# Seven more pieces of the sample rows' attention values split into a rounded part and its rest, one per prompt column, on one Trainium2 core

## What is computed

```python
def cross_attention(h, mem_k, mem_v, w_q, w_o):
    B, T, _ = h.shape
    q = jnp.einsum('btd,de->bte', h, w_q).reshape(B, T, XA_HEADS, XA_HD)
    s = jnp.einsum('bthd,bmhd->bhtm', q, mem_k.astype(h.dtype)).astype(jnp.float32) * (XA_HD ** -0.5)
    p = jax.nn.softmax(s, axis=-1).astype(h.dtype)
    o = jnp.einsum('bhtm,bmhd->bthd', p, mem_v.astype(h.dtype)).reshape(B, T, D_MODEL)
    return jnp.einsum('btd,de->bte', o, w_o)
```

## Time and profile before

| | us |
|---|---|
| median of 3 runs | 1855.91 |
| lowest, highest | 1854.45, 1859.5 |
| the profiled execution | 1854.26 |
| its span, first to last instruction | 1851.9 |
| TensorE busy in the span | 1814.0 |
| VectorE busy | 1150.0 |
| ScalarE busy | 796.2 |
| mean granted TensorE clock | 0.998 of full |

### The profile page before, as it was taken

One profiled execution on the slowest core, in us unless ns is written; L12 is line 12 of the kernel. 1 busy time (PEld: TensorE's weight loads), 2 busy tenths in 40 slices (PEclk: granted clock), 3 DMA queues, 4 the chain that ended last, 5 costly groups with the idle time before them and its releaser, 6 DMA issues.

```text
span 1851.9 us, 34219 instructions
## 1 busy us (share of the span) xinstructions
PE 1814.0 (98%) x13818; PEld 1723.1 (93%) x13818; DVE 1150.0 (62%) x1573; ACT 796.2 (43%) x842; POOL 183.2 (10%) x185
## 2 busy tenths in 40 slices
PE   8999999999999999999999999999999999999997
PEld 6999999988999999888749999999999999999997
DVE  6888447746766577555676656666544566665443
ACT  6454545343363533443642344443333444443344
POOL 5000000002106300000005500000000000000231
PEclk9999999999999999999999999999999999999999
DMA  8555554472045667797784688886456899984553
GB/s 266 162 166 174 180 167 155 137 241 76 17 154 177 216 211 247 276 311 250 251 283 128 190 239 249 250 249 193 129 183 193 239 249 248 249 225 134 170 187 110
DMA packets 415128, 367.19 MB, mean 198 GB/s; under 512 B 11519, under 2 KB 374014, under 8 KB 414486
## 3 DMA queue, kind: packets, MB, share of 16 engines
q1 hardware_dynamic: 387368, 340.76, 60.0%
q10 hardware_dynamic: 27678, 25.26, 4.2%
HBM read 347.84 MB, written 18.35 MB: 198 GB/s over the span
## 4 chain that ended last, share of the span: by engine, by line
PE 89%; DVE 5%; ACT 2%; issue 1%; POOL 1%; DMA 1%; DVEq 0%; ACTq 0%; POOLq 0%
PE ps L467 65%; PE ps L543 9%; PE ps L524 4%; DVE w_lo L446 2%; PE ps L961 1%; PE ps L510 1%; PE ps L1245 1%; ACT w_hi L439 1%; PE ps L1260 1%; PE ps L1163 1%; PE ps L1084 1%; PE ps L1402 1%; DMA gst<-in_state_gla_dram 1%; PE ps L1448 1%; PE ps L1440 1%
## 5 line engine op out<-in xcount | busy, mean ns | idle before, releaser
L439 ACT ACTIVATE w_hi<-raw 128x2048 fp32r<-128x2048 f32 (+1 forms) x285 | 512.3, 1797 | 857.6 <-PE ps L467 709.9
L446 DVE TENSOR_TENSOR w_lo<-raw,w_hi 128x2048 fp32r<-128x2048 f32 (+1 forms) x285 | 620.1, 2176 | 261.3 <-ACT w_hi L439 258.1
L467 PE MATMUL ps<-act_hi,w_lo 128*128 128x264 f32 x2560 | 732.8, 286 | 6.2 <-DVE w_lo L446 4.1
L467 PE MATMUL ps<-act_lo,w_hi 128*128 128x264 f32 x2560 | 725.4, 283 | 0.0
L467 PE MATMUL ps<-act_hi,w_hi 128*128 128x264 f32 x2560 | 724.9, 283 | 0.0
L467 PEld LDWEIGHTS ps<-act_hi,w_lo 128*128 128x128 f32 x2560 | 482.2, 188 | 10.6 <-issue 3.9
L467 PEld LDWEIGHTS ps<-act_lo,w_hi 128*128 128x128 f32 x2560 | 482.5, 188 | 0.4
L467 PEld LDWEIGHTS ps<-act_hi,w_hi 128*128 128x128 f32 x2560 | 480.0, 187 | 0.0
L467 PE MATMUL ps<-ff_hi,w_lo 128*128 128x264 f32 x704 | 201.1, 286 | 0.0
L467 PE MATMUL ps<-ff_hi,w_hi 128*128 128x264 f32 x704 | 200.1, 284 | 0.0
L467 PE MATMUL ps<-ff_lo,w_hi 128*128 128x264 f32 x704 | 199.4, 283 | 0.0
(11 more groups left out here) (444 smaller groups left out, 2172.9 us busy)
## 6 DMA issues: line engine op xcount, KB each, us to landing
raw<-in_w_in_dram SPq DMA_DIRECT2D x56, 1024.0 KB, 7.5
raw<-in_ffn_w_gate_dram SPq DMA_DIRECT2D x44, 1024.0 KB, 5.7
raw<-in_ffn_w_up_dram SPq DMA_DIRECT2D x44, 1024.0 KB, 5.7
raw<-in_ffn_w_down_dram SPq DMA_DIRECT2D x32, 768.0 KB, 4.8
raw<-in_ffn_w_down_dram SPq DMA_DIRECT2D x32, 640.0 KB, 6.1
raw<-in_w_out_dram SPq DMA_DIRECT2D x16, 1024.0 KB, 6.3
raw<-in_xa_w_q_dram SPq DMA_DIRECT2D x16, 1024.0 KB, 6.7
raw<-in_xa_w_k_dram SPq DMA_DIRECT2D x16, 1024.0 KB, 6.3
```

What stands on the lines that cost most here:

```text
L439: act.activation(w_part(ph, w_hi[b]), raw_part(ph, r, half), ACT.Copy)\
L446: dve.tensor_tensor(w_part(ph, w_lo[b]), raw_part(ph, r, half), w_part(ph, w_hi[b]), ALU.subtract)\
L467: mm = pe.matmul(ps[:, acc(ph, u), 0:ph.cols], w[b][:, k, :], v[:, kk + k, 0:ph.cols], start=first and k == 0 and m == 0, stop=last and k ...
```

## The change

`HALVED` goes from 18 to 25, so pieces 18 to 24, the first seven of the tail, take the split form too; a new name, `EARLY_HALVED`, keeps the old 18. VectorE no longer makes the rounded copy `ow_hi` of the 16 prompt tiles: ScalarE does, in a loop over j of its own. For each j that loop has `first_values(18 + j)`, a wait for `att_o` (tile j summed by TensorE), the copy `ow_hi`, and for j up to 6 `high_values(18 + j)`. VectorE waits for that copy before `ow_lo`, and for j up to 6 does `low_values(18 + j)` behind it. The copy of `orow` now stands at j = 15 of ScalarE's loop.

```diff
--- before.py
+++ after.py
@@ -59,7 +59,8 @@
 EARLY_PIECES = 14
 RING = 8
 PIECES = 2 * NB * XH
-HALVED = 18
+EARLY_HALVED = 18
+HALVED = 25
 ACC_CREDIT = 4
 
 
@@ -2031,13 +2032,18 @@
                         high_values(2 * (n - 39) + v)
                 if n == 3 * KT - 1:
                     keep_rows(3, 1)
-            for v in range(18, NB * XH):
-                if v == 20:
+            for j in range(KT):
+                if j == 2:
                     split(*unit_at(3 * KT + 1))
-                first_values(v)
-            W(act, "s_o", NB * XH)
-            act.activation(orow[:, :], ps[0:NB * XH, 6, :], ACT.Copy).then_inc(rows_copied, 1)
-
+                if j < 14:
+                    first_values(18 + j)
+                if j == KT - 1:
+                    W(act, "s_o", NB * XH)
+                    act.activation(orow[:, :], ps[0:NB * XH, 6, :], ACT.Copy).then_inc(rows_copied, 1)
+                W(act, "att_o", j + 1)
+                act.activation(ow_hi[:, j, 0:T], ps[:, 4 + j % 2, 0:T], ACT.Copy).then_inc(v_halved, 1)
+                if EARLY_HALVED + j < HALVED:
+                    high_values(EARLY_HALVED + j)
             run("x_o", none, "gu0")
             act.wait_ge(new_rows_kept, 32)
             run_with_pieces(0, gate_take, "dn0")
@@ -2634,7 +2640,7 @@
 
             def low_values(n):
 
-                dve.wait_ge(v_halved, n + 1)
+                dve.wait_ge(v_halved, n + 1 + max(n + 1 - EARLY_HALVED, 0))
                 r = (NB * XH + n - EARLY_PIECES) % RING
                 dve.tensor_tensor(ring_r[r][:, 0, :], ring[r][:, 0, :], ring_r[r][:, 1, :], ALU.subtract).then_inc(v_mixed, 1)
 
@@ -2685,8 +2691,10 @@
                        .then_inc(N["s_oe"], 1)
                 W(dve, "att_o", j + 1)
                 src = ps[:, 4 + j % 2, 0:T]
-                link(dve.tensor_copy(ow_hi[:, j, 0:T], src))
+                dve.wait_ge(v_halved, EARLY_HALVED + j + 1 + min(j, HALVED - EARLY_HALVED))
                 dve.tensor_tensor(ow_lo[:, j, 0:T], src, ow_hi[:, j, 0:T], ALU.subtract).then_inc(N["att_oe"], 1)
+                if EARLY_HALVED + j < HALVED:
+                    low_values(EARLY_HALVED + j)
 
             def new_state(half, i):
```

## The result

| us | before | with the change |
|---|---|---|
| median | 1855.85 (6 runs) | 1868.96 (6 runs) |
| lowest, highest | 1854.45, 1859.5 | 1866.37, 1870.15 |
| the profiled execution | 1854.26 | 1866.37 |
| its span | 1851.9 | 1864.7 |

The ratio of the times is 1.0072, with a 95% interval of 1.0062 to 1.0082: the change makes the kernel slower.

The account below looks back on a forecast made before the run. TensorE, busy 1814.0 of 1851.9 us, was taken to bound the kernel. Closed steps, the unit split and the end, less gains, made 11.2 us; 1855.91 + 11.2 = 1867.1 us, range 1863 to 1871.5, chance 0.67.

Parts of the forecast that it names:

- the loop: Tail, split pieces: rest, piece, tile, tile copy and rounded copy wait in a ring over three engines, 3.39 us against 2.04.
- sum at the full clock: Whole tail: `x_o` starts at 983.45 instead of 972.25, 11.2 us later, with no fall of TensorE's clock counted.
- the rest 0.74: VectorE's rest of a piece until TensorE starts its sum: 0.69 for one plus 0.05 for the signal.
- The unknown step: ScalarE's tile copy until its next instruction starts, not shown in the trace: 0.31 us taken, upper end 0.59.
- The step with the unit split: From piece 19 to piece 20, where both halves of the split of unit 49 stand inside the ring: 5.75 us.
- The end: `orow` copied behind tile 14's copy: turns start at 982.0, 11.3 us later; `x_o` at 983.45, a 0.15 wait gone.
- the cover of 0.07 us: From tile 7 on, unsplit pieces: values take 3.03 us, TensorE comes to the sum after 3.10, so no cost.
- the bound for a slow tile copy: ScalarE's tile copy at 0.59 us: each closed step costs 0.28 more, the whole 13.8 instead of 11.2, or 1869.7 us.
- a case that I gave 0.27: Rival: TensorE's clock falls in the 4.1 us break between pieces 19 and 20, adding 1.6 to 4.8; 1868.7 to 1871.9 us.
- the prediction's own sign: The forecast would be wrong if, among other signs, TensorE's granted clock fell in 947 to 952 us.
- the break at 453 to 456 us: Mid-program before the change: TensorE busy 0.60 of 3 us with the clock at 1.00; cited as its longest break there.
- The basis: Forecast added to before's median, 1855.91 us, giving 1867.1; the profiled execution's 1854.26 would give 1865.4.

Follow-up runs that it names:

- the turned order: The change with each piece's rounded copy and rest put ahead of the tile's copy and rest in each j, same engines; median 1862.06 us against 1856.04 before.
- the copy back on VectorE: The change with the rounded copy of the tiles made on VectorE again instead of ScalarE; median 1865.06 us against 1856.31 before.
- the filler kernel: The change plus six f32 matmuls, result unread, in TensorE's long wait behind tile 2; median 1864.20 us against 1856.31 before.
- the tile copy only: The change without its seven split pieces (`HALVED` 18), ScalarE still copying the 16 tiles; median 1857.71 us against 1856.31 before.
- three pieces: The change with three split pieces (18 to 20) instead of seven, `HALVED` 21; median 1862.21 us against 1855.13 before.

## Why the prediction was right

In short: the loop, its place and its size were right. The number was helped by two errors that cancel, a sum at the full clock that was 1.4 us too long and a fall of the clock that it left out, and that part is luck.

**The mechanism held, with its place and its size.** The loop through rest, piece, tile, tile copy and rounded copy was worked out at 3.39 us; it measures 3.23. By parts: the rest 0.74 (956.59 to 957.33) as taken, the two matmuls 0.48 instead of 0.52, the tile 1.06 instead of 1.16 (its four matmuls take 1.02 us where they took 1.13 at the full pace of before; why is open), the tile copy 0.28 instead of 0.31, the rounded copy 0.66 as taken. The unknown step, the tile copy, was well placed at its lower end. The experiment with the turned order shows that it is the order, and the one with the copy back on VectorE that it isn't the engine.

**The step with the unit split** was 5.75 in the prediction and 5.61 in the trace.

**The end.** The copy of `orow` behind tile 14 put the turns 2.08 us behind the start of tile 14 in the prediction, and so it measures, 1.02 more than before. I had `x_o` start 1.06 us behind tile 15's start; it started after 0.78. Steps of the tail from tile 7 on were 2.04 us, as costed, so the cover of 0.07 us was enough.

**The sum at the full clock was too long by 1.4 us**: 11.2 against 9.8 (the filler kernel). Five steps at 0.16 less are 0.8 of it, the unit step 0.14, the end from tile 14 on 0.3; the rest is in the first piece and in the stretch from tile 7 on. In the change's own trace 11.03 stands against 11.2, and so close a match is luck, since 1.25 of the 11.03 is the clock. Two slips in the working had no weight. By its own terms `x_o` starts at 983.42 and not 983.45. And the bound for a slow tile copy doesn't follow from its parts: 0.28 for the start, five steps and the end are 2.0, with 7 x 0.2 it is 3.4, so 14.6 and not 13.8; the copy was at the lower end anyway.

**The clock: a case that I gave 0.27, and took for the less likely.** It came true, and by the prediction's own sign the forecast was wrong there: the clock was not to fall in 947 to 952, and 952.3 in the profile after is 950.7 there, since the tail began 1.6 us later. The measured median also lies in that rival's range (1868.7 to 1871.9). I let myself be led by the break at 453 to 456 us, behind which the clock had stayed at 1.00. That row was one draw. In the profile of the kernel with the tile copy only, the same break in the same code has this behind it:

```profile
454.00:456.00 2.00, 0.18 (x2) 0.00 (x0) 1.93 (x6) 1.99 (x4) 0.00 (x0) 1.00 0.92 309
...
458.00:460.00 2.00, 2.00 (x12) 2.00 (x11) 1.22 (x2) 0.60 (x1) 0.00 (x0) 0.50 1.10 351
```

In every profile that holds the 4.1 us wait without a filler the clock fell (the change, `orow` ahead of tile 14, the turned order, three pieces), and also right behind the 3.52 us of the copy back on VectorE; in none of the kernels whose waits in the tail stay below 2 us did it fall in the tail. The Trainium skill, "TensorE: Matmul & The Clock Gate", section "What's actually happening", has the halved clock after idle time, and these traces agree (0.50 in 953 to 955 behind the wait of 4.10 us). Its price was put at 1.6 us for each slow j, one to three of them. It was 1.25 for one: the piece took 0.86 instead of 0.48 (952.85 to 953.71), and tile 3 was seen after 1.94 instead of 1.06 (953.71 to 955.65).

**The basis.** I took the median and not the profiled execution for the basis, and the profiles suggest why that was right. Before's profile has no fall of the clock between 0 and 1838 us; the change's has one at 504 to 508 besides the one in the tail, in code that is the same in both. Before, the same stretch:

```profile
504.00:506.00 2.00, 2.00 (x18) 2.00 (x19) 1.83 (x9) 0.00 (x0) 0.00 (x0) 1.00 0.00 0
506.00:508.00 2.00, 2.00 (x20) 2.00 (x20) 0.23 (x1) 1.27 (x3) 0.00 (x0) 1.00 0.00 0
```

Of the ten later profiles nine have a fall between 454 and 462, and two of them a second one at 506 to 511. Each costs 1.5 to 1.6 us. The profiled execution of before had none, and the 1.6 us between the two profiles that arose ahead of the tail are this. The times of the other runs go with the clock too. Of before's runs beside the experiments, those with a mean granted clock of 0.998 took 1853.4 to 1854.4 us and those with 0.995 took 1856.1 to 1858.0. The six runs of the change go from 1866.37 us at 0.996 to 1870.15 at 0.992.

Of the 13.1 us between the medians, the tail of the profile accounts for 11.0, which is a little below the interval of the ratio (11.5 to 15.2 us). So about 2 us aren't in the 11.2 that was forecast. The lower clock of the change's runs points at more or longer falls than its profile has; where in the program they lie isn't shown.

## What to carry to other kernels

Before work is moved onto engines with room, write down for one turn of the loop what each moved instruction waits for and what is queued behind it: here two copies that wait for TensorE were put ahead of what TensorE waits for, and 0.5 us of gain for each piece turned into 1.2 us of loss, while the same work one piece earlier in the queues gained. The sum of the busy times tells the limit (1.6 us for a step here), the order whether it is reached (3.23, 2.38, 1.60 us with nearly the same work). And here a wait of TensorE of some 4 us cost more than itself, by what ran behind it at the low clock: 1.25 us where the clock came back after one step, 2.2 to 2.5 where it stayed low for two.

## What the runs showed of the hardware

- The clock fell to 1.2 GHz around the end of TensorE's waits of 3.5 and 4.1 us, each time (five kernels): 0.3 to 1.3 us before the end of the four waits of 4.1, and 0.4 us after the one of 3.5. Filling 2.7 us of the 4.1 with matmuls whose result nobody reads kept 2.4 GHz and made the tail 1.25 us shorter.
- After a wait of 2.4 us (453 to 456) the clock fell in 9 of 12 profiles, and after one of 2.0 (501 to 504) in 3 of 12, in the same code. A single profile in which it holds is no evidence that it always does. The runs of one kernel lie up to 5 us apart, and the slower ones are those with the lower mean clock.
- The low clock lasted for one step in the change (952.3 to 955.7) and for two with the copy back on VectorE (953.8 to 960.3) and with three pieces (951.3 to 958.1). The fall cost 1.25 us in the first, 2.2 and 2.5 in the others. What decides how long it lasts isn't shown.
